# Router logits on repeated columns, plain products as fillers, and gathered rows added by GpSimd

## What is computed

```python
def moe_swiglu(h, w_router, w_gate, w_up, w_down):
    t = h.reshape(b * l, d)
    logits = jnp.matmul(t, w_router)                  # 8 experts
    top_val, top_idx = lax.top_k(logits, TOP_K)       # 2 of them
    gates = jax.nn.softmax(top_val, axis=-1)
    combine = jnp.sum(one_hot(top_idx, N_EXPERTS) * gates[..., None], axis=1)
    out = jnp.zeros((b * l, d))
    for e in range(N_EXPERTS):
        out = out + combine[:, e:e + 1] * swiglu(t, w_gate[e], w_up[e], w_down[e])
    return out
# x = x + moe_swiglu(rmsnorm_2(x, moe_norm_w), ...); return rmsnorm_2(x, final_norm_w)
```

## Time and profile before

| | us |
|---|---|
| median of 3 runs | 1845.68 |
| lowest and highest of them | 1844.6, 1846.19 |
| the profiled execution | 1844.57 |
| its span, first to last instruction | 1842.9 |
| TensorE busy in the span | 1814.3 |
| VectorE busy | 1500.6 |
| ScalarE busy | 1269.6 |
| GpSimd busy | 118.4 |

### The profile page before, as it was taken

How to read it: one execution, slowest core, us unless ns; L and a number is a source line. 1 busy time by engine, 2 the same in 40 slices (tenths; PEclk the granted TensorE clock), 3 DMA queues, 4 the chain that set the end, 5 groups by cost and what they waited for, 6 DMA issues and landing times.

```text
span 1842.9 us, 27066 instructions
## 1 busy us (share of the span) xinstructions
PE 1814.3 (98%) x9202; PEld 1535.1 (83%) x9202; DVE 1500.6 (81%) x1857; ACT 1269.6 (69%) x1659; POOL 118.4 (6%) x214
## 2 busy tenths in 40 slices
PE   9999999999999999989999999999999999999997
PEld 7888788888888899878888888888888888888886
DVE  6686777777666788685899999999999999999998
ACT  5645565556544666675778778787787787877876
POOL 2040040000000000150100000000000000000100
PEclk9999999999999999999999999999999999999999
DMA  8424568563655455415799999999999999999994
GB/s 329 156 95 138 180 190 323 183 201 115 192 198 164 159 189 191 169 40 190 271 405 352 407 379 372 390 352 410 378 364 402 356 395 382 362 407 372 375 413 174
DMA packets 239642, 512.47 MB, mean 278 GB/s; under 512 B 11036, under 2 KB 58490, under 8 KB 239498
## 3 DMA queue, kind: packets, MB, share of 16 engines
q1 hardware_dynamic: 235634, 493.08, 73.2%
q0 software_dynamic: 3808, 18.38, 2.6%
q10 hardware_dynamic: 144, 0.26, 0.0%
HBM read 505.38 MB, written 12.07 MB: 281 GB/s over the span
## 4 chain that ended last, share of the span: by engine, by line
PE 92%; DVE 5%; issue 1%; ACT 1%; DMA 0%; DVEq 0%; SPq 0%; ACTq 0%
PE ps L261 24%; PE ps L263 24%; PE ps L262 24%; PE ps L2328 9%; PE ps L2331 4%; PE ps L2589 1%; DVE w_lo L254 1%; PE ps L2169 1%; PE ps L2569 0%; DVE arena L1784 0%; PE ps L2092 0%; PE ps L2384 0%; ACT w_hi L245 0%; PE ps L2113 0%; PE ps L2539 0%
## 5 line engine op out<-in xcount | busy, mean ns | idle before, releaser
L254 DVE TENSOR_TENSOR w_lo<-raw,w_hi 128x1024 fp32r<-128x1024 f32 x938 | 1102.9, 1225 | 140.9 <-ACT w_hi L245 140.0
L245 ACT ACTIVATE w_hi<-raw 128x1024 fp32r<-128x1024 f32 x938 | 941.9, 1056 | 254.5 <-PE ps L263 241.4
L261 PE MATMUL ps<-w_hi,a 128*128 128x512 f32 (+1 forms) x1216 | 480.7, 395 | 1.7 <-DVE w_lo L254 0.9
L263 PE MATMUL ps<-w_hi,a 128*128 128x512 f32 (+1 forms) x1216 | 472.8, 389 | 0.0
L262 PE MATMUL ps<-w_lo,a 128*128 128x512 f32 (+1 forms) x1216 | 471.9, 388 | 0.0
L261 PE MATMUL ps<-w_hi,a_hi 128*128 128x512 f32 (+1 forms) x720 | 280.4, 389 | 1.6 <-DVE a_lo L1937 1.0
L263 PE MATMUL ps<-w_hi,a_lo 128*128 128x512 f32 (+1 forms) x720 | 278.7, 387 | 0.0
L262 PE MATMUL ps<-w_lo,a_hi 128*128 128x512 f32 (+1 forms) x720 | 278.6, 387 | 0.0
L261 PEld LDWEIGHTS ps<-w_hi,a 128*128 128x128 f32 x1216 | 228.5, 188 | 49.2 <-DVE w_lo L254 2.2
L263 PEld LDWEIGHTS ps<-w_hi,a 128*128 128x128 f32 x1216 | 228.2, 188 | 48.1
L262 PEld LDWEIGHTS ps<-w_lo,a 128*128 128x128 f32 x1216 | 228.6, 188 | 44.4
(11 more groups left out here) (376 smaller groups left out, 1434.3 us busy)
## 6 DMA issues: line engine op xcount, KB each, us to landing
raw<-in_moe_w_gate_dram SPq DMA_DIRECT2D x112, 1024.0 KB, 6.5
raw<-in_moe_w_up_dram SPq DMA_DIRECT2D x112, 1024.0 KB, 7.3
raw<-in_moe_w_down_dram SPq DMA_DIRECT2D x112, 1024.0 KB, 5.6
raw<-in_ssd_w_in_dram SPq DMA_DIRECT2D x24, 1024.0 KB, 5.0
raw<-in_w_ffn_in_dram SPq DMA_DIRECT2D x22, 1024.0 KB, 5.0
raw<-in_w_in_dram SPq DMA_DIRECT2D x21, 1024.0 KB, 6.2
raw<-in_w_ffn_out_dram SPq DMA_DIRECT2D x11, 1024.0 KB, 5.0
raw<-in_dense_w_gate_dram SPq DMA_DIRECT2D x11, 1024.0 KB, 5.0
```

Source lines behind the costliest of these rows:

```text
L245: nc.scalar.activation(w_hi[:, u % SPL, part], raw[:, u % RAW, part], ACT.Copy).then_inc(hi_done, 1)
L254: last = nc.vector.tensor_tensor(w_lo[:, u % SPL, part], raw[:, u % RAW, part], w_hi[:, u % SPL, part].bitcast(F32), ALU.subtract)
L261: nc.tensor.matmul(o, lh, rh, start=start, stop=False, skip_group_check=True)
L263: return nc.tensor.matmul(o, ll, rh, start=False, stop=stop, skip_group_check=True)
```

## The change

Three edits. First, the logits' product takes the 8 columns of the router's weights 16 times over, so that it writes 128 columns; VectorE reads the first 8 of each tile, and the counts move to column 256. Second, three plain products of the identity are put in ahead of the second tile's transposes, and the 18 filler transposes become nine plain products. Third, the additions of the gathered rows go from VectorE to GpSimd, directly behind the transfers that bring the rows; VectorE waits for them before it adds the last task's result.

```diff
                 for n in range(2):
                     for t in range(T):
                         nc.gpsimd.indirect_dma_start(y_back[n][t], None, result_rows, ...)
+                pool.wait_ge(y_in, 16 * 2 * T)
+                for n in range(2):
+                    if n:
+                        pool.wait_ge(rows_added, T)
+                    for t in range(T):
+                        nc.gpsimd.tensor_tensor(x[:, t, :], x[:, t, :], y_back[n][t], ALU.add).then_inc(rows_added, 1)
...
-                    last = nc.vector.tensor_scalar(lg[:, t], ps[4][:, t * NE:(t + 1) * NE], rstd[:, t:t + 1], None, ALU.mult)
+                    last = nc.vector.tensor_scalar(lg[:, t], ps[4][:, t * P:t * P + NE], rstd[:, t:t + 1], None, ALU.mult)
...
-                    count = ps[4][:, 64:64 + NE]
+                    count = ps[4][:, S:S + NE]
...
                     split_lo(dve, M0 + 4, n)
-                    if not more:
-                        rows_add(0)
                     product_lo(n, 4)
...
-                def rows_add(n):
-
-                    dve.wait_ge(y_in, 16 * 2 * T)
-                    for t in range(T):
-                        last = nc.vector.tensor_tensor(x[:, t, :], x[:, t, :], y_back[n][t], ALU.add)
-                    C.link(last)
...
                 task_lo(n_last, False)
-                rows_add(1)
                 result_lo(n_last)
+                dve.wait_ge(rows_added, 2 * T)
                 scatter_add()
...
+            def stream(bank, n):
+
+                for _ in range(n):
+                    nc.tensor.matmul(ps[bank][:, 0:P], ident, ident, start=True, stop=True)
...
                 for t in range(T):
+                    if t:
+                        stream(3, 3)
                     pe.wait_ge(x_new, UPD["ssd"] - 2 + 2 * t)
...
-                        last = nc.tensor.matmul(ps[4][:, t * NE:(t + 1) * NE], m_xT[:, c, t * P:(t + 1) * P], wr[:, c, :],
+                        last = nc.tensor.matmul(ps[4][:, t * P:(t + 1) * P].rearrange("p (n e) -> p n e", e=NE),
+                                                m_xT[:, c, t * P:(t + 1) * P], bcast(wr[:, c, :], 1, P // NE),
                                                 start=(c == 0), stop=(c == DC - 1), skip_group_check=True)
...
-                busy(6, 18)
+                stream(6, 9)
...
-                nc.tensor.matmul(ps[4][:, 64:64 + NE], ones, sel[:, 0:NE], start=True, stop=False)
-                nc.tensor.matmul(ps[4][:, 64:64 + NE], ones, sel[:, NE:2 * NE], start=False,
+                nc.tensor.matmul(ps[4][:, S:S + NE], ones, sel[:, 0:NE], start=True, stop=False)
+                nc.tensor.matmul(ps[4][:, S:S + NE], ones, sel[:, NE:2 * NE], start=False,
                                  stop=True).then_inc(r_rank, 1)
```

More of the change, by code:

```diff
@@ L577, in block_kernel @@
         rows_idx, y_out, y_in = sem("rows_idx"), sem("y_out"), sem("y_in")
+        rows_added = sem("rows_added")
         pool_in, s_moe_g = sem("pool_in"), sem("s_moe_g")
```

## The result

| | before | changed |
|---|---|---|
| median of 20 runs | 1844.13 us | 1849.88 us |
| lowest to highest | 1841.69 to 1846.19 | 1847.11 to 1853.49 |
| span of the profiled execution | 1842.9 | 1847.0 |

The ratio is 1.0032, 95% interval 1.0026 to 1.0038: slower by 5.8 us by the medians, clear of the noise and beyond 0.2%. The prediction gave +5.3 and 1851.0. (The kernel before was run again beside it; its 20 runs have a median 1.5 us under that of the first three.)

A forecast was written before the change was run, and what follows sets the result against it. TensorE was taken as the bound, busy 942.64 of 942.70 us in the expert stage. Router +0.4, end -1.1 and additions +6.0 made +5.3 us on a median of 1845.68, so 1851.0, range 1845.0 to 1853.3.

The forecast's parts named there:

- the turns between GpSimd and VectorE: Last task's first step: GpSimd's additions and VectorE's weight splits lock each other out, costing VectorE 8.9 us in all.
- Price of a turn: Last task's first step: each 128x1024 GpSimd addition takes 2.43 us and costs VectorE 2.2 us.
- the timetable: Last task: three units' splits reach TensorE 0.4, 4.1 and 1.3 us late, 5.8 in sum, 6.0 with 0.2 for the clock.
- the logits' 0.119 us a record: Router: 32 logits records on 128 columns take 3.8 us at 2.4 GHz, so VectorE starts 1.05 us earlier.
- the fillers out of the way: Router: nine plain products take 2.1 us and no longer hold up the rank products, delayed some 0.8 us before.
- VectorE's scaling of the second tile: Router, behind the selection: this 1.28 us becomes what is late next, leaving a gain of 1.3 us.
- the dip in the gather: Router: after a 3.0 us pause TensorE runs the gather at 1.2 GHz, costing 1.7 us; held 2 in 3 likely.
- End: After 1823 us: the last low part no longer waits for VectorE's additions, gaining 1.1 us, bounds 0.9 to 1.3.
- (a): Rival, router: as forecast but no 1.2 GHz stretch in the gather, +3.6 us, 1849.3; chance 0.26.
- (b): Rival, last task: GpSimd's additions cost nothing that reaches TensorE, -2.4 us (1843.3) or -0.7 (1845.0); chance 0.10.
- (c): Rival, router: usually 1.2 GHz reached 3 us into the old gather, so the change saves 1.5 us more; chance 0.08.
- (d): Rival, last task: TensorE's stop and clock loss add up in full, +8 us, 1853.5; chance 0.06.

The follow-up runs named there:

- Experiments 1 and 7: 1: kernel before with only the additions moved to GpSimd, 1850.59 us, ratio 1.0034; 7: changed kernel with GpSimd memsets in place of the additions, 0.9993.
- experiment 6: Changed kernel with only the first two additions on GpSimd, the other two on VectorE behind its last split; ratio 1.0006 to the kernel before.
- experiment 9: Router edits with additions spread on VectorE, plus fillers: 12 plain products for 9 ahead of the rank products, 3 more behind; 1841.59 us, 0.9984 of the kernel before.
- the version with pieces: Changed kernel with each GpSimd addition cut into four of 128x256; ratio 1.0011 to the kernel before.

## Why the prediction was right

- **Where**: it placed the loss in the turns between GpSimd and VectorE in the last task's first step. Experiments 1 and 7 show it: the edit alone gives 1.0034, and with memsets at the same place, which read nothing, no loss is left.
- **Price of a turn**: 2.2 us for each of four, from a row of a quarter of the size and one of half. Measured 2.2 (3.43 - 1.22) for three, and 1.6 for the fourth, which began under the 0.68 us instruction that doesn't take part: 8.2 in place of 8.9.
- **How much reaches TensorE**: the timetable said 0.4, 4.1, 1.3 late, and 6.0 with the clock. Measured 0.33 and 3.63 idle, then 1.2 GHz, and no third stop, because TensorE at half speed came to the third unit when it was ready. With 0.3 us beyond the idle time for each stop (experiment 6) and 1.7 for the dip this is 6.3 us, and measured is +6.2 over the undisturbed tasks (+6.0 over the one profile of before). The mechanism was the forecast one, but the parts were not: 4.0 of idle where 5.8 of lateness was forecast, and 1.7 of clock where 0.2 was added. That they meet within 0.2 us is in part luck.
- **Router**: the logits' 0.119 us a record, the fillers out of the way, VectorE's scaling of the second tile as what is late next, and the dip in the gather all came. The gather started 1.7 us earlier in place of 1.3: the rank was read at 876.12, right behind the scaling, and the logits came 0.1 us sooner. So the sum was -0.1 in place of +0.4, the one part off by more than 0.2 us. That the gather would dip was put at 2 in 3 by a comparison with one row; other executions show no dip behind that same pause (last section), so the row was weaker evidence than it was taken for.
- **End**: -1.3 for -1.1, at the edge of the bounds given.
- **The total**: the parts forecast +5.3 and the two profiles give +4.6; the medians give +5.8. The 1851.0 stood on the median of three runs, 1.5 us above that of twenty. The range holds the result by either.
- **The rivals**: (a), no dip, did not happen in any of the seven profiled executions with nine fillers (or 18 transposes) and wide logits, and experiment 9 shows what it takes. (b) is refuted. Of (c) nothing is seen in the two profiles with the router of before (gather 3.81 us). (d) did not come: the dip lay over the third unit's lateness.

## What to carry to other kernels

Before work is given to an idle GpSimd, look at what VectorE does at that moment: if its instructions have two SBUF inputs and GpSimd's reads SBUF, the time isn't hidden but taken from VectorE almost one for one (2.2 us for each addition here). What VectorE can spare is its slack against the engine that waits for it, not its idle share. An addition that stalls the path by 1 us can be moved a step earlier on its own engine, one at a time, where the slack makes it up. A gain ahead of a pause of TensorE can be lost to the clock behind it, as the router's was; here it paid to fill the pause.

## What the runs showed of the hardware

- A GpSimd memset of 128x1024 float32 takes 0.96 us and slows no split (1.22); an addition of the same size makes them 3.43.
- A GpSimd addition of 128x256 that ran nearly free took 0.74 us in place of the 0.61 worked out. None of 128x1024 ran free: the first took 2.57 us in place of 2.43, but it began while a split ran to 1737.06 and ended 2.27 us behind it, so some of it may be wait.
- One cause of the scatter of the runs can be seen. Ahead of the router, in code that no version touches, a dip of 1.2 GHz comes or doesn't: in the additions alone there are two (221 and 436), in the kernel before one, in the version with pieces none, behind the same pause of 2.04 us. The router starts at 864.5 us without a dip, between 865.7 and 866.7 in the eight profiles with one, and between 867.5 and 867.8 in the three with two; half of some 3.4 us at 1.2 GHz is an estimate of 1.7 us for each. First the pieces, then the additions alone:

```profile
434.00:437.30 3.30, 3.30 (x19) 2.94 (x18) 0.64 (x1) 0.00 (x0) 0.00 (x0) 1.00 0.34 120
```

```profile
221.00:223.00 2.00, 2.00 (x5) 1.56 (x6) 1.89 (x4) 2.00 (x4) 0.00 (x0) 0.50 0.00 0
436.00:438.00 2.00, 2.00 (x6) 1.55 (x6) 0.00 (x0) 0.00 (x0) 0.00 (x0) 0.50 0.07 25
```

- So whether a given pause brings a dip is not fixed. The gather's came in all seven profiled executions with nine fillers (or 18 transposes) and wide logits, a pause of 3 us with four pairs of small products in it. What decides stays open.
